# A layer's conditioning sums moved from VectorE to TensorE: 32-partition quarters of a PSUM bank in a two-layer transformer kernel

## The reference

```
m = silu(c) @ w + b                      # w: 1024 x 3072, one per half layer
shift, scale, gate = split(m, 3);  gate = 1 + gate
h = x * (1 + scale) + shift
y = mixer(h)                             # or the squared-relu MLP
x = layer_norm(ALPHA * x + gate * y)     # then the next half's shift and scale
```

## Time and profile before

| | |
|---|---|
| median of the runs | 1525.03 us |
| the profiled execution, its span | 1525.93 us, 1523.9 us |
| PE matmul busy | 1357.9 us, 89% |
| PE weight load busy | 1206.9 us, 79% |
| DVE busy | 1044.0 us, 69% |
| ACT busy | 598.5 us, 39% |
| POOL busy | 2.9 us |
| DMA | 262.90 MB, mean 173 GB/s |

### The profile page before, as it was taken

The page is one execution under the profiler, slowest core; times in us unless marked ns, Lnnn a source line. Parts: engine busy times, 40 slices in busy tenths (PEclk is TensorE's granted clock), DMA queues, the critical chain, the costliest instruction groups (busy, mean ns, idle before and its releaser), DMA issues.

```text
span 1523.9 us, 22456 instructions
## 1 busy us (share of the span) xinstructions
PE 1357.9 (89%) x8718; PEld 1206.9 (79%) x8718; DVE 1044.0 (69%) x1478; ACT 598.5 (39%) x800; POOL 2.9 (0%) x5
## 2 busy tenths in 40 slices
PE   3875889999898788999959997999996899999997
PEld 3753679999797677999849986899986676899996
DVE  6979788777777757766676785755568645575554
ACT  1424333343344424333345322534336453353332
POOL 0000000000000000000000000000000000000000
PEclk9898889999899998999979998999999999999999
DMA  9653438877375334655516430455452310454540
GB/s 357 262 184 106 153 116 328 315 268 257 122 266 185 132 111 181 231 215 191 203 48 224 139 111 28 166 193 191 171 189 107 135 63 29 166 208 175 188 160 28
DMA packets 45841, 262.90 MB, mean 173 GB/s; under 512 B 5191, under 2 KB 6855, under 8 KB 21066
## 3 DMA queue, kind: packets, MB, share of 16 engines
q1 hardware_dynamic: 32672, 216.88, 39.2%
q10 hardware_dynamic: 13102, 45.09, 8.5%
HBM read 260.90 MB, written 1.05 MB: 172 GB/s over the span
## 4 chain that ended last, share of the span: by engine, by line
PE 73%; DVE 17%; ACT 4%; issue 3%; DMA 2%; ACTq 0%; DVEq 0%; SPq 0%
PE banks L530 21%; PE banks L531 21%; PE banks L532 21%; DVE w_lo L1496 3%; DMA A<-ada_w 2%; PE banks L737 2%; PE banks L998 2%; PE banks L694 1%; ACT A L1053 1%; ACT w_hi L1037 1%; DVE A L1516 1%; DVE hT_lo L1485 1%; PE banks L640 1%; DVE A L1505 1%; DVE mx L1602 1%
## 5 line engine op out<-in xcount | busy, mean ns | idle before, releaser
L1496 DVE TENSOR_TENSOR w_lo<-raw,w_hi 128x2048 fp32r<-128x2048 f32 x193 | 439.8, 2287 | 160.4 <-ACT w_hi L1037 158.1
L1037 ACT ACTIVATE w_hi<-raw 128x2048 fp32r<-128x2048 f32 x193 | 368.8, 1913 | 246.4 <-PE banks L532 211.6
L530 PE MATMUL banks<-hT_hi,w_hi 128*128 128x256 f32 x1432 | 414.0, 289 | 7.6 <-DVE hT_lo L1485 3.3
L532 PE MATMUL banks<-hT_hi,w_lo 128*128 128x256 f32 x1432 | 410.2, 286 | 0.0
L531 PE MATMUL banks<-hT_lo,w_hi 128*128 128x256 f32 x1432 | 410.1, 286 | 0.0
L530 PEld LDWEIGHTS banks<-hT_hi,w_hi 128*128 128x128 f32 x1432 | 280.2, 196 | 13.5 <-issue 7.4
L531 PEld LDWEIGHTS banks<-hT_lo,w_hi 128*128 128x128 f32 x1432 | 280.1, 196 | 3.3 <-issue 1.0
L532 PEld LDWEIGHTS banks<-hT_hi,w_lo 128*128 128x128 f32 x1432 | 279.7, 195 | 0.0
L530 PE MATMUL banks<-w_hi,R 128*128 128x512 f32 (+1 forms) x592 | 231.2, 390 | 3.9 <-DVE R L1485 3.6
L531 PE MATMUL banks<-w_lo,R 128*128 128x512 f32 (+1 forms) x592 | 229.3, 387 | 0.0
L532 PE MATMUL banks<-w_hi,R 128*128 128x512 f32 (+1 forms) x592 | 228.7, 386 | 0.0
(11 more groups left out here) (221 smaller groups left out, 1329.1 us busy)
## 6 DMA issues: line engine op xcount, KB each, us to landing
raw<-stream SPq DMA_DIRECT2D x193, 1024.0 KB, 4.8
A<-ada_w ACTq DMA_DIRECT2D x73, 512.0 KB, 5.4
A<-ada_w SPq DMA_DIRECT2D x16, 512.0 KB, 9.8
A<-ln_g ACTq DMA_DIRECT2D x4, 512.0 KB, 4.0
A<-ln_b ACTq DMA_DIRECT2D x4, 512.0 KB, 5.5
A<-ada_w SPq DMA_DIRECT2D x1, 1536.0 KB
A<-x_t SPq DMA_DIRECT2D x2, 512.0 KB, 12.4
X<-ada_w SPq DMA_DIRECT2D x1, 1024.0 KB
```

The lines of the kernel that those rows point to most:

```text
L530: pe.matmul(o, lh, rh, start=start, stop=False, skip_group_check=True)
L532: return pe.matmul(o, ll, rh, start=False, stop=stop, skip_group_check=True)
L1037: act.activation(w_hi[:, s, :], raw[:, s, :], ACT.Copy).then_inc(hi_done, 1)
L1496: v.tensor_tensor(w_lo[:, s, :], raw[:, s, :], w_hi[:, s, :], ALU.subtract).then_inc(lo_done, 1)
```

## The change

The weighted sums of s = 0 (shift, scale and gate) and of s = 1 (shift and scale) are made by TensorE. For each slice and each 512 columns one matmul has the silu(c) column, repeated 32 times, as its stationary operand and the slice as its moving one, and adds into a quarter (32 partitions) of one PSUM bank: four quarters hold the 2048 values of shift and scale, two those of the gate. The bias enters first, in the same quarters, by a matmul over one partition. ScalarE copies the bank to SBUF (`row_out`), and 16 matmuls over one partition each turn the rows into columns in four banks (`row_columns`). The gate is spread from one row of each quarter. VectorE's parts of this are gone, as are GpSimd's clearing of the accumulator and VectorE's clearing of the gate's. The gate's slices are taken in another order and at other steps. The eight slices of s = 1 stand in the attention steps 1 to 8, 1 MB each, in two pairs of buffers, their loads issued by ScalarE two ahead. Besides, the tables of angles are made before the first projection; the first weight unit is loaded before the last four slices, and its low part is made before `finish(0)`; unit 3 is loaded without a wait.

```diff
+        mod_rows = {0: arena(ADAC, 512), "gate": arena(ADAC + 512, 512), 1: arena(HTF + 1536, 512)}
+        row_bank = {0: 4, "gate": 5, 1: 2}
+        next_bias = arena(ADAC + D, 2 * D)[0:1, :]
+        row_w = [[arena(ADAW, D), arena(ADAW + D, D)], [arena(ADAW + 2 * D, D), arena(ADAC, D)]]
...
-            s += [("angles",), ("gate_sum", 0, 0, 1, 5, 6)]
             s += fills(AB + 2, "T", "h", "rope", [AB_TMP])
             s += [("turn2", cq, COL["ab_q"], "cq_ab", 0)] + rest(AB + 4)
             s += fills(AB + 3, "T", "h", "rope", [AB_TMP])
...
-            s += rope(4) + [("gate_sum", 4, 2)] + rest(AB + 5)
+            s += rope(4) + [("gate_sum", 0, 5, 6, 0, 1)] + rest(AB + 5)
             f = fills(AB + 4, "T", "cq_ab", "rope", [AB_TMP] * 4)
-            s += [f[0]] + rope(6) + rest(AB + 6) + [("gate_sum", 5, 3), f[1]] + rope(12) + [("gate_sum", 6, 4), f[2]]
-            s += rope(14) + rest(AB + 7) + [("gate_sum", 7, 7), f[3]] + rope(8) + [("gate0",)]
...
-            s += fills(AB + 5, "T", "h", "rope", [AB_TMP]) + some(2) + rope(10)
+            s += [f[0]] + rope(6) + rest(AB + 6) + [("gate_sum", 4, 2, 3), f[1]] + rope(12) + [("gate_sum", 6, 4, 7), f[2]]
+            s += rope(14) + rest(AB + 7) + [f[3]] + rope(8) + [("gate0",)]
+            s += fills(AB + 5, "T", "h", "rope", [AB_TMP]) + rope(10)
             s += [("index", h) for h in range(3)] + rest(AB + 8)
-            s += fills(AB + 6, "T", "h", "rope", [AB_TMP]) + some(2) + rope(0)
+            s += fills(AB + 6, "T", "h", "rope", [AB_TMP]) + rope(0)
             s += [("index", h) for h in range(3, IDX_HEADS)] + rope(2) + rest(AB + 9)
...
-                s += some(1)
+                if 1 <= i <= KT:
+                    s += [("ada_row", i - 1)]
                 if i == 6:
                     s += rest(AB + 10)
-            s += some(len(ada_parts)) + [("rows", 0, 0)]
-            return s + downs(AB + 7, [0, 1, 2, 3], {0: whole(1, 6), 1: whole(1, 7)})
+            s += [("rows", 0, 0)]
+            return s + downs(AB + 7, [0, 1, 2, 3], {0: [("row_out", 1)]})
...
             for i in range(2 * KT):
                 load_start(i)
-            load(0, 0)
+                if i == KT + 3:
+                    load(0, 0)
...
-            load(1, 1)
-            load(2, 2)
-            sp.wait_ge(ada_used, adas_before(0, KT))
-            load(3, 3)
+            for u in range(1, SLOTS):
+                load(u, u)
...
-        @block.gpsimd
-        def _(pool):
-            pool.wait_ge(ada_col, 1)
-            pool.memset(ada_acc, 0.0).then_inc(pool_zero, 1)
...
+            def bias_rows(b, row, n_):
+
+                for q in range(n_):
+                    m = pe.matmul(B[b][32 * q:32 * q + 32, :], ones[0:1, 0:32], row[0:1, 512 * q:512 * q + 512], start=True,
+                                  stop=False, skip_group_check=True)
+                return m
+
+            def slice_rows(b, q0, k, w):
+
+                for q in range(2):
+                    at = 32 * (q0 + q)
+                    m = pe.matmul(B[b][at:at + 32, :], silu_c[:, k:k + 1].to_broadcast([P, 32]), w[:, 512 * q:512 * q + 512], start=False,
+                                  stop=k == KT - 1, skip_group_check=True)
+                return m
+
+            def row_columns(s_):
+
+                pe.wait_ge(row_ready, {0: 1, 1: 3}[s_])
+                for j in range(4):
+                    for q in range(4):
+                        r = slice(32 * q, 32 * q + 1)
+                        m = pe.matmul(B[q][:, j:j + 1], mod_rows[s_][r, P * j:P * j + P], ones[r, 0:1], start=True, stop=True,
+                                      skip_group_check=True)
+                m.then_inc(ada_col, 1)
+                for q in range(4):
+                    held[q] = (col_ready, s_ + 1)
+
             def gate(first=False):
 
                 if n["y"]:
                     pe.wait_ge(y_read, n["y"] - 2)
                 if first:
-                    pe.wait_ge(gate_used, KT)
-                acc = gate_r if first else ada_acc[:, 2 * D:3 * D]
+                    pe.wait_ge(row_ready, 2)
                 for h in range(2):
+                    if first:
+                        r = slice(32 * h, 32 * h + 1)
+                        m = pe.matmul(B[6 + h][:, :], ones[r, :], mod_rows["gate"][r, :], start=True, stop=True)
+                        continue
+                    acc = ada_acc[:, 2 * D:3 * D]
                     m = pe.matmul(B[4 + h][:, :], ones[:, :], acc[:, 512 * h:512 * h + 512], start=True, stop=True)
                 m.then_inc(gate_ps, 1)
                 n["gates"] += 1
...
                 elif kind == "finish":
 
-                    claim(3)
                     if a[0] == 0:
                         pe.wait_ge(ld_bias, 16)
+                        bias_rows(row_bank[0], start_bias, 4).then_inc(bias_col, 1)
+                        pe.wait_ge(silu_ready, 1)
+                        for part in range(2):
+                            for k in range(KT):
+                                pe.wait_ge(ld_start[k], 16 * (part + 1))
+                                slice_rows(row_bank[0], 2 * part, k, START_BUF(A, k)).then_inc(ada_used, 1)
+                        row_columns(0)
+                    elif a[0] == 1:
+                        for q in range(4):
+                            claim(q)
+                        row_columns(1)
+                    else:
+                        claim(3)
+                        pe.wait_ge(ada_used, adas_before(a[0], KT))
                         for j in range(2 * KT):
-                            m = pe.matmul(B[3][:, j:j + 1], start_bias[:, P * j:P * j + P], ones[0:1, 0:1], start=j == 0,
-                                          stop=False, skip_group_check=True)
-                        m.then_inc(bias_col, 1)
-                    for j in range(2 * KT):
-                        if a[0] == 0 and j % KT == 0:
-                            pe.wait_ge(ada_used, j + KT)
-                        elif j == 0:
-                            pe.wait_ge(ada_used, adas_before(a[0], KT))
-                        m = pe.matmul(B[3][:, j:j + 1], ada_acc[:, P * j:P * j + P], ones[:, 0:1], start=a[0] > 0,
-                                      stop=True, skip_group_check=True)
-                    m.then_inc(ada_col, 1)
-                    held[3] = (col_ready, a[0] + 1)
+                            m = pe.matmul(B[3][:, j:j + 1], ada_acc[:, P * j:P * j + P], ones[:, 0:1], start=True, stop=True,
+                                          skip_group_check=True)
+                        m.then_inc(ada_col, 1)
+                        held[3] = (col_ready, a[0] + 1)
+                elif kind == "gate_sum":
+                    if a[0] == 0:
+                        pe.wait_ge(ld_gate, 16 * (len(gate_bufs) + 1))
+                        bias_rows(row_bank["gate"], gate_r, 2)
+                    for i, k in enumerate(a[1:]):
+                        for h in range(2):
+                            m = pe.matmul(B[row_bank["gate"]][32 * h:32 * h + 32, :],
+                                          silu_c[:, k:k + 1].to_broadcast([P, 32]), gate_w[k][:, 512 * h:512 * h + 512], start=False, stop=a[0] + i == KT - 1, skip_group_check=True)
+                        m.then_inc(gate_used, 1)
+                elif kind == "ada_row":
+                    k = a[0]
+                    if k == 0:
+                        claim(2)
+                        pe.wait_ge(ld_bias, 32)
+                        bias_rows(row_bank[1], next_bias, 4)
+                        held[2] = (row_ready, 3)
+                    for part in range(2):
+                        pe.wait_ge(ld_rows[part][k % 2], 16 * (k // 2 + 1))
+                        slice_rows(row_bank[1], 2 * part, k, row_w[k % 2][part]).then_inc(ada_used, 1)
...
+            def load_row(k):
+
+                for part in range(2):
+                    if k >= 2:
+                        act.wait_ge(ada_used, adas_before(1, k - 2, part + 1))
+                    act.dma_start(row_w[k % 2][part], ada_w[1, k, :, D * part:D * part + D]).then_inc(ld_rows[part][k % 2], 16)
+
+            def row_out(s_):
+
+                r = slice(0, 64 if s_ == "gate" else P)
+                act.activation(mod_rows[s_][r, :], B[row_bank[s_]][r, :], ACT.Copy).then_inc(row_ready, 1)
...
+            act.dma_start(gate_r[0:1, :], ada_b[0:1, 2 * D:3 * D]).then_inc(ld_gate, 16)
+            act.wait_ge(ang_ready, 1)
+            for i, dst in enumerate((sinT, cosT)):
+                ins = act.activation(dst[:, :], arena(ANGLES + SEQ * (2 + i), SEQ), ACT.Sin)
+            ins.then_inc(trig_done, 1)
             hi(0, 0, 1)
             for step in STEPS:
                 kind, a = step[0], step[1:]
                 if kind == "finish" and a[0] == 0:
+                    act.wait_ge(ada_used, adas_before(0, KT))
+                    row_out(0)
...
                 elif kind in ("gate", "gate0"):
-                    gate_rows(4)
```

(33 more changed lines are left out.)

47 lines of the change are left out of this document (14 added, 33 removed).

## The result

The changed kernel takes 1516.15 us (median of five runs, 1515.13 to 1517.61) against 1525.49 us for the kernel before, run beside it on the same chip: a ratio of 0.9932, 95% interval 0.9920 to 0.9945. A second session gave 0.9935 (0.9918 to 0.9953). It is faster by 9.3 us in the medians and 10.4 by the ratio, where 12.2 were forecast.

The account below looks back on a forecast made before the run. VectorE was taken as the fuller engine from 34 to 155 us. Start +2, projections -13, attention -1.5 and boundary +0.3 sum to -12.2 from 1525.9, so 1513.7, given as 1513 us; range 1505 to 1529.

Parts of the forecast that it names:

- Price of a quarter matmul: TensorE's new 32-column fp32 matmuls: 0.45 us each, bounds 0.23 (four at once) and 0.9 (no overlap); 90 make 41 us.
- L707's pattern: Existing 64-column tiles on alternating bank halves, overlapping by about half; the basis for 0.45 us a quarter matmul.
- Rival (b): All summing stages: quarters don't overlap, 0.9 us each; 1536 us, 23.6 over the forecast; chance 0.11.
- break-even of 0.67 us: All 90 new matmuls: from 0.67 us each the kernel is slower by more than 0.5%.
- Start: 0 to 38 us, to the first projection matmul: +2 us, bounds -2 to +9.
- rival (a): Start: TensorE stays at 1.2 GHz while it sums; start +9 instead of +2, 1522 us; chance 0.17.
- Projections: Projections and index, 38 to 125 us: VectorE loses work and waiting, -13 us, bounds -17 and -6.
- a clock that no longer drops: Projections: part of the lower bound of -17 us, beside 2.5 us of slices; not in the -13.
- Rival (c): Projections: transfers of unit 6 and the gate's slices decide and halve the gain; 1519 us; chance 0.12.
- Attention: 125 to 180 us: steps 0 to 3 -4.1, steps 4 to 9 +2.6, sum -1.5 us, bounds -5 and +5.
- Three of the four slices count with about 1.2: Attention steps 0 to 3: VectorE slices removed there gain 4.1 us; the fourth stands beside TensorE's first scores.
- Boundary: Output projection and norm: first transposes wait for VectorE's four small operations in `finish(1)`, +0.3 us (0 to 0.6).

Follow-up runs that it names:

- e2: The changed kernel with SyncE asking for weight unit 6 ahead of the gate's slices instead of behind them: 1514.77 us.
- e5: The changed kernel with both halves of each slice summed into one 32-partition quarter, same count of matmuls, half the sums left wrong: 1530.22 us, ratio 1.0030 to the kernel before.
- e4: The changed kernel with the sixteen column matmuls going row by row, four from one 32-row group, then four from the next: 1515.62 us.
- e3: The changed kernel with bias rows and slice 0 of the second modulation moved into TensorE's 7.6 us wait for VectorE's diagonals: 1512.99 us.
- e1: The changed kernel with the second modulation's columns and finish(1) ahead of the last two units of the output projection: 1517.58 us.
- e9: The changed kernel with the moves of e8 and e3, and finish(1) between the halves of the residual's second tile: 1511.64 us.
- e10: As e9, with the gate's spread also behind the first three index heads: 1509.96 us, ratio 0.9893 to the kernel before.
- e11: As e10, with slice 1 of the second modulation beside slice 0 in the gap of step 1: 1509.36 us, ratio 0.9894 to the kernel before.
- e7: Only the first modulation on TensorE, angles ahead of it; gate and second modulation on VectorE as in the kernel before: 1522.88 us.
- e8: The changed kernel with unit 5's projection matmuls ahead of the two that spread the gate: 1516.25 us.
- e6: First modulation and gate on TensorE as in the change, the second modulation back on VectorE as in the kernel before: 1520.55 us.

## Why the prediction was right, and which terms were off

The direction, the mechanism and the mark at the first maxima were right: 113.06 us, "near 112" forecast (114 by its own terms, +2 and -13 from 125.2, since the 112 leaves out the +2). VectorE's load left the projections and TensorE became the bound, which e2 shows by taking away the longest other wait for nothing. The forecast's marks on the way: first ropes at 65 (66.3), the gate's spread ending at 84.5 (84.3), rope 10 at 91 (its first operation ran ahead at 84.2, the one that needs TensorE at 92.7, 12.1 us earlier than before), the output projection by 172 (167.5). The sum, -12.2, against -10.7 at the last split and -9.3 in the medians. That the sum came so close is in part luck: the terms were off by -4.2, +3.1, +1.6 and +1.0 us, and the first hides most of the rest. By its terms:

- **Price of a quarter matmul**: 0.45 us taken, 0.23 to 0.9 as bounds. Measured at the high clock (but for e5's first matmuls): 0.48 with two quarters in turn (gate; 0.52 with the tail at the start), 0.25 with four (attention), 0.86 to 0.90 with one (e5). L707's pattern was the right neighbour for two. That four quarters follow each other within one slice of the second modulation was in the code and I did not use it; it halves the attention's bill. The loads of 32 columns that the prediction priced at 27 ns each, two per matmul, are in the trace, two per matmul at 105 to 108 ns (high clock), and take no time of their own: in the row at 130.59 us all eight of a slice lie in its first 0.16 us. Rival (b) has its direction confirmed by e5, which is slower than the kernel before (1530), but not its size (1536, or 23.6 us over the forecast against 14 over the change): the start cost 2.2 and not 4.5, and the attention 4.4 and not 11, where e5 still alternates between two quarters. Its break-even of 0.67 us counts every matmul as exposed; no run has that price throughout.
- **Start**: +2 taken, -2.2 measured. 3.6 us for sixteen columns was the wrong row: 1.07 measured, and e4 shows how much of it is the rotation (2.47 without). The other 1.7 us of the +2 were a margin for a slow clock. The clock was slow only for the first two slices, where the transfers hide it, and here for two of the last four (granted 0.78 over 28:32 us), so that the last four took 5.6 us where the second session's took 4.9; rival (a), slow throughout, is out. The last slice, taken to land at 29.5, started at 29.9 here and at 29.1 in the second session, where TensorE waited for it. But the absolute marks in the projections had been worked out from 37.8, and the units there ran on to the same times: a start 2.2 us earlier and a stage that is 3.1 us less improved than forecast are one error with two signs.
- **Projections**: -13 taken, -9.9 measured in this profile, -11.6 in the second. 1.6 us of the difference is the clock, unit 5's above all. The stage's own comparison with the kernel before is blurred in the same way: before, about 44 fp32r matmuls of it ran at half clock, here 15, an estimate of 2.7 us, for which the forecast's -13 has no term (it stands in its lower bound, "a clock that no longer drops"). Rival (c), the transfers, had the wait and its place right (unit 6 at 60.8 forecast, 60.2 measured) and its price wrong: e2 removes it and gains nothing.
- **Attention**: -1.5 taken, +0.1 measured. Here a step failed: "Three of the four slices count with about 1.2". In step 1 TensorE does what VectorE waits for, after a wait of its own and at half clock; the bias and slice 0 stand in front of the scores of pair 2, and 3.7 us of them show. e3 moves them and gets back 3.6. (Nor does the -4.1 come out of its parts: three times 1.2 is 3.6, and nothing is said of the other 0.5.) The forecast treated a stage's busy sums (22.7 under 21.8 and 3.1) as if the work could lie anywhere in it. From the first maxima to the fifth the stage gained 0.2 us where 4.1 were forecast. Steps 4 to 9 went the other way, because a slice costs 1.0 and not 1.8: 6.1, 5.1 and 5.6 for the last three steps between maxima, where 5.5 to 6 were forecast, 0.3 us more in all than before and not 2.6.
- **Boundary**: +0.3 taken (to 0.6), +1.3 measured. The wait was named but priced at `finish(1)`'s four operations (0.7 us); what it waits for is that VectorE does them after the whole residual, and the transposes come out cold (1.94 us against 1.07). e1 and e9 move it and gain 3.0 and 2.4 at the last split, 2.3 and 1.5 by the later mark: still more than was lost, since the kernel before also had the columns' `finish` in that chain.

## To carry to other kernels

A sum over rows on TensorE into 32-partition quarters pays only while neighbouring matmuls go to different quarters: here that alone is the difference between 10 us gained and 4 lost. When work moves to another engine, put it by that engine's waits and not by its busy share: the bias and slice 0 placed behind a wait of 7.6 us cost 3.7, inside it nothing. A part's worth read from one profile needs the clock beside it: here the low clock moved by 3 us of work from one variant to the next. A mark taken at an operation that the variant itself moves says too much (3.0 us for 2.3). And the longest wait of a stage may be worth nothing (4.5 and 11.7 us here), so delete it once before building a theory on it.

## What the runs showed of the hardware

- Fp32 matmuls with 32 columns of weights and 512 to stream: 0.90 us each in one quarter (the gate's in e5), 0.48 with two quarters in turn, 0.25 with four. The Trainium skill, "TensorE: Matmul & The Clock Gate", section "Part 3: Packing small matmuls", has three column tiles at 2.38 times the speed of one; four give 3.6 here (0.90 / 0.25). These tiles share a row group, for which that section has no overlap of weight loads; this case's trace differs. The loads take 105 to 108 ns each, two per matmul, and the eight of one slice lie within 0.16 us beside the matmuls (the rows at 130.59 us).
- Sixteen matmuls with a contraction over one partition and one column to stream: 1.07 us when each takes another row group than the last, 2.47 when four in turn share one.
- One code has two outcomes in TensorE's clock. After the same instructions, unit 5 or 6 (48 matmuls, 5.8 us at the high level) was begun at a granted 0.50 to 0.68 or at 1.00; in pairs of profiles of the same code this made 1.6 us (the change) and 3.7 us (e10 and e11, alike up to there). Moving the wait in front of it moved the place of the low clock, from unit 5 to unit 6, and did not remove it.
- The first projection matmul of kernels with the change's own start comes between 34.8 and 38.3 us. In eleven profiles it comes 4.65 to 4.66 us after the last slice matmul ends (6.03 in e4, by the columns; 5.67 in e7, by a slow cast, see below), and that end follows the landing of the transfers and the clock behind TensorE's wait of 2.72 us: the last four slices took 4.9 us in the second session of the change and 6.49 in e8 (granted 0.50 over 28:32 us).

```profile
27.17 6.49 PE L828 MATMUL banks<-A,silu_c 128*32 128x512 f32 x16 [2.72 <-DMA A<-ada_w]
```

- In e7, as in the kernel before, GpSimd clears VectorE's accumulator as soon as the columns are done, and here that falls on VectorE's first cast of the split. The cast took 1.44 us, where the same one took 0.43 in the change, which has no clearing, and 0.43 in e6, which has it later. That is one sighting, and no run was made for it. In the kernel before, the unit's `low` stood in that place and took its usual 2.28 us.

```profile
33.25 2.66 POOL L511 MEMSET A<- 128x3072 f32 x1 [32.80 <-PE banks L847]
...
34.75 1.44 DVE L1520 CAST hT_hi<-A 128x512 fp32r<-128x512 f32 x1 [1.16 <-ACT A L1228]
```
